# Token-mixer projections as pairs of seven block products in a one-core diffusion trunk layer

## What is computed

```python
h = rmsnorm(x, norm_mix) * (1.0 + sc1) + sh1          # sc1, sh1 ... from silu(cond) @ w_ada + b_ada
proj = h @ w_in                                       # 640 x 1024 by 1024 x 3584
xr, gr, q_raw, ff, fb, iv, og = split(proj)           # seven groups of 512 columns
...   # xr: convolution, two LRU scans;  q, ff, fb, iv, og: HGRN2, four heads of 128 columns, two directions
y = concatenate([y_lru, y_hg]) @ w_out
x = x + g1 * y
x = x + g2 * expert_choice_ffn(rmsnorm(x, norm_ffn) * (1.0 + sc2) + sh2)   # 16 experts, 3 x 4 MB of weights each
```

## Time and profile before

| what | value |
|---|---|
| median of 3 runs (lowest, highest) | 959.01 us (957.84, 960.46) |
| the profiled execution: its time, its span | 958.34 us, 956.6 us |
| DVE, ACT, POOL busy in the span | 54%, 30%, 11% |
| loads issued by SyncE and ScalarE | 253.77 MB on q1 of 276.15 MB in all |
| mean DMA rate over the span | 289 GB/s |

### The profile page before, as it was taken

One profiled execution on the slowest core, in us unless ns is written; L12 is line 12 of the kernel. 1 busy time (PEld: TensorE's weight loads), 2 busy tenths in 40 slices (PEclk: granted clock), 3 DMA queues, 4 the chain that ended last, 5 costly groups with the idle time before them and its releaser, 6 DMA issues.

```text
span 956.6 us, 19027 instructions
## 1 busy us (share of the span) xinstructions
PE 928.8 (97%) x8298; PEld 423.3 (44%) x8298; DVE 516.9 (54%) x1269; ACT 289.7 (30%) x507; POOL 101.2 (11%) x115
## 2 busy tenths in 40 slices
PE   5999999999999999999999999999999999999996
PEld 4555756768667554463222222222222223333332
DVE  4487667663654743764464461752636516444096
ACT  5137756564653824323020100200202002010103
POOL 3200010000000022112102002011020110100100
PEclk9999999999999999999999999999999999999999
DMA  9991014404029443168999999999999999999993
GB/s 333 334 386 52 2 55 157 160 5 176 10 92 367 174 164 150 66 240 323 403 399 404 408 416 408 415 401 413 418 405 413 405 413 425 401 426 413 412 380 122
DMA packets 52930, 276.15 MB, mean 289 GB/s; under 512 B 4400, under 2 KB 12752, under 8 KB 39920
## 3 DMA queue, kind: packets, MB, share of 16 engines
q1 hardware_dynamic: 45744, 253.77, 66.1%
q0 software_dynamic: 5584, 15.89, 5.7%
q10 hardware_dynamic: 1520, 5.28, 1.4%
HBM read 261.91 MB, written 13.01 MB: 287 GB/s over the span
## 4 chain that ended last, share of the span: by engine, by line
PE 79%; DMA 8%; DVE 5%; ACT 3%; issue 3%; POOL 0%; SPq 0%; POOLq 0%; DVEq 0%; ACTq 0%
PE pa L699 44%; PE p L699 34%; DMA ring<-in_w_up_dram 3%; DMA reg_e<-in_w_up_dram 3%; DMA ring<-in_w_ada_dram 1%; ACT reg_c L1374 1%; ACT L1374 1%; ACT reg_d L1374 1%; DMA reg_c<-h_rows,row_s 0%; ACT reg_b L1374 0%; DVE reg_a L2246 0%; DVE reg_b L1867 0%; PE p L854 0%; DVE reg_a L2241 0%; DVE reg_b L1838 0%
## 5 line engine op out<-in xcount | busy, mean ns | idle before, releaser
L699 PE MATMUL pa<-ring,reg_b 128*32 128x512 f32 (+1 forms) x1696 | 250.0, 593 | 0.7 <-DMA ring<-in_w_up_dram 0.5
L699 PE MATMUL p<-ring,reg_b 128*16 128x512 f32 (+1 forms) x1920 | 215.3, 592 | 1.1 <-issue 1.1
L699 PE MATMUL pa<-reg_a,ring 128*128 128x512 f32 (+1 forms) x640 | 191.2, 453 | 2.2 <-DVE reg_a L1730 1.5
L699 PEld LDWEIGHTS pa<-ring,reg_b 128*32 128x32 f32 (+1 forms) x1696 | 82.5, 117 | 143.7 <-issue 142.6
L699 PEld LDWEIGHTS pa<-reg_a,ring 128*128 128x128 f32 x640 | 98.3, 191 | 80.1 <-issue 79.9
L699 PEld LDWEIGHTS p<-ring,reg_b 128*16 128x16 f32 (+1 forms) x1920 | 63.9, 102 | 143.9 <-issue 143.9
L2142 DVE STREAM_TRANSPOSE reg_b<-reg_b 32x128 f32<-32x128 f32 x384 | 116.3, 303 | 5.9
L2158 DVE TENSOR_TENSOR reg_b<-reg_b,pa 128x512 f32<-128x512 f32 x16 | 11.0, 686 | 146.7 <-PE pa L699 146.4
L1374 ACT ACTIVATE reg_b<-pa 128x512 f32<-128x512 f32 (+1 forms) x20 | 12.4, 619 | 239.8 <-PE pa L699 239.8
L1374 ACT ACTIVATE reg_b<-reg_d,x_mod 128x128 f32<-128x128 f32 (+1 forms) x112 | 39.4, 440 | 140.7 <-PE p L699 140.7
L1374 ACT ACT_TABLE_LOAD x57 | 73.1, 1283 | 4.6 <-issue 2.8
(11 more groups left out here) (335 smaller groups left out, 937.4 us busy)
## 6 DMA issues: line engine op xcount, KB each, us to landing
ring<-in_w_gate_dram SPq DMA_DIRECT2D x25, 2048.0 KB, 21.1
ring<-in_w_down_dram SPq DMA_DIRECT2D x24, 2048.0 KB, 24.1
ring<-in_w_up_dram SPq DMA_DIRECT2D x22, 2048.0 KB, 21.5
ring<-in_w_ada_dram SPq DMA_DIRECT2D x8, 2048.0 KB, 8.5
ring<-in_w_in_dram SPq DMA_DIRECT2D x6, 2048.0 KB, 19.9
ring<-in_w_ada_dram SPq DMA_DIRECT2D x8, 1024.0 KB, 12.8
reg_a<-in_w_up_dram SPq DMA_DIRECT2D x4, 2048.0 KB, 20.3
reg_a<-in_w_gate_dram SPq DMA_DIRECT2D x3, 2048.0 KB, 18.1
```

The source lines that it names most:

```text
L699: return nc.tensor.matmul(out, lhsT, rhs, start=start, stop=stop, **kw)
```

## The change

- **Pairs.** The last two items of FILL[0] to FILL[5] (always feature items: Q and OG, or FF and FB) form a pair, `TWOS`. The pair's 256 columns, cut in two, by 1024 features, cut in two, and the 640 tokens, cut in two halves of 320, are multiplied as 2 x 2 blocks with seven products in place of eight (Winograd's form). A product is 4 matmuls of 320 columns into one PSUM bank, the first 320 of its 512 columns.
- **Token sums.** GpSimd makes four sums or differences of quarters of `hT` (128 x 1280 each), once, right behind its copy of the prompt tokens, which no longer waits behind the LRU state. They lie in slots 2 and 3 of the ring, which hold no weights of `w_in` any more.
- **Weight sums.** VectorE makes four of them a pair (128 x 512 each, SBUF to SBUF): those of pairs 0 and 1 behind the LRU's second scan, those of pair u + 2 at the end of unit u.
- **Joins.** ScalarE copies the first and second product (128 x 320 each, PSUM to SBUF) behind its logarithm. VectorE makes seven 320-wide adds: the first in front of the weighings, the other six behind them and ahead of the head's output, the ada bias, the state updates and the masks. Five of the seven read PSUM. In even units ScalarE then applies Silu in place, behind the key copy.
- **TensorE's order** in a pair: products 1 and 2, [first ada sum], 3, 4, 5, 6, [second ada sum and `turn_k`, in an order that depends on the unit], 7. The head norm of units 2 and 4 stands behind product 4. The `ada_turn` follows.
- **Values first.** EARLY is now the V item of head 1; FILL[1] keeps FF and FB, and in units 3 and 5 the V item comes in front of the pair.
- **Loads.** Those weights come as cells of 128 columns (0.5 MB, rows of 512 B) into slots 5, 0 and 1; each is used again when its column is free, and SyncE waits in between for TensorE's items and for earlier cells to land.
- The slot of `a2[0]` is moved, and two semaphores of the routing become one; nothing else behind unit 5 changes.

```diff
-         (("in", IN_Q), 5), (("in", IN_OG), 0), (("in", IN_FF), 1), (("in", IN_FB), 2), (("in", IN_V), 3)]
+         (("head", 5), 5), (("head", 0), 0), (("head", 1), 1), (("sums", 0), 2), (("sums", 1), 3)]
...
+HEAD0 = [(IN_Q, 0), (IN_OG, 0), (IN_FF, 0), (IN_FB, 0), (IN_V, 0)]
+EARLY = (IN_V, 1)
 FILL = []
 for _h in range(1, HEADS):
-    FILL += [[(IN_Q, _h), (IN_OG, _h)], [(IN_FF, _h), (IN_FB, _h), (IN_V, _h)]]
+    FILL += [[(IN_Q, _h), (IN_OG, _h)], ([(IN_V, _h)] if _h > 1 else []) + [(IN_FF, _h), (IN_FB, _h)]]
+TWOS = [fill[-2:] for fill in FILL]
 FILL += [[(IN_GR, 0), (IN_GR, 1)], [(IN_GR, 2), (IN_GR, 3)]]
-HEAD0 = [(IN_Q, 0), (IN_OG, 0), (IN_FF, 0), (IN_FB, 0), (IN_V, 0)]
-EARLY = FILL[1].pop(0)
...
+        mixing = ring[:, 2:4, :, :].rearrange("p s k n -> p (s k n)")
+        x_sum = [mixing[:, m * 4 * HALF:(m + 1) * 4 * HALF].rearrange("p (k t) -> p k t", k=4) for m in range(4)]
+        w_sum = [[mixing[:, 16 * HALF + (3 * b + m) * 512:16 * HALF + (3 * b + m + 1) * 512].rearrange("p (k n) -> p k n", k=4)
+                  for m in range(3)] for b in range(2)]
+        x_quarter = [[hT[:, 4 * kh:4 * kh + 4, HALF * th:HALF * (th + 1)] for kh in range(2)] for th in range(2)]
+        banks = [pa[n // 2][:, 512 * (n % 2):512 * (n % 2) + HALF] for n in range(4)]
...
+            for g in (IN_Q, IN_OG, IN_FF, IN_FB):
+                cell_load(g, 0)
+            sp_eng.wait_ge(freed[0], 1)
+            cell_load(IN_V, 0)
+            cell_load(IN_Q, 1)
+            cell_load(IN_OG, 1)
+            cell_load(IN_V, 1)
+            sp_eng.wait_ge(freed[1], 1)
+            cell_load(IN_FF, 1)
+            cell_load(IN_FB, 1)
+            cell_load(IN_Q, 2)
+            cell_load(IN_OG, 2)
+            whole_load("ada", 4)
+            sp_eng.wait_ge(full, 3)
+            cell_load(IN_FF, 2)
+            sp_eng.wait_ge(full, 4)
+            cell_load(IN_FB, 2)
+            sp_eng.wait_ge(full, 5)
+            cell_load(IN_V, 2)
+            sp_eng.wait_ge(full, 6)
+            cell_load(IN_V, 3)
+            whole_load("ada", 5)
+            whole_load("ada", 6)
+            sp_eng.wait_ge(two_ps, 7)
+            sp_eng.wait_ge(*cells_by((IN_V, 3)))
+            cell_load(IN_Q, 3)
+            cell_load(IN_OG, 3)
+            sp_eng.wait_ge(*cells_by((IN_OG, 3)))
+            cell_load(IN_FF, 3)
+            cell_load(IN_FB, 3)
+            for c in range(7, 12):
+                whole_load("ada", c)
+            whole_load("in", IN_GR)
+            whole_load("out", 0)
+            whole_load("out", 1)
...
             pool.wait_ge(h_mod, MIXED)
             pool.wait_ge(xt_dve, NT + MIXED)
             nc.gpsimd.tensor_copy(hT_p[:, :, :], hT[:, :, TS:T]).then_inc(pool_step, 1)
+            pool.wait_ge(freed[2], 1)
+            pool.wait_ge(freed[3], 1)
+            nc.gpsimd.tensor_tensor(x_sum[0], x_quarter[1][0], x_quarter[1][1], ALU.add).then_inc(mixed, 1)
+            nc.gpsimd.tensor_tensor(x_sum[2], x_quarter[0][0], x_quarter[1][0], ALU.subtract).then_inc(mixed, 1)
+            pool.wait_ge(mixed, 2)
+            nc.gpsimd.tensor_tensor(x_sum[1], x_sum[0], x_quarter[0][0], ALU.subtract).then_inc(mixed, 1)
+            pool.wait_ge(mixed, 3)
+            nc.gpsimd.tensor_tensor(x_sum[3], x_quarter[0][1], x_sum[1], ALU.subtract).then_inc(mixed, 1)
...
+            def product(i, bank, w, x):
+                for k in range(4):
+                    r = mm(banks[bank], w[:, k, :], x[:, k, :], k == 0, k == 3)
+                r.then_inc(two_ps, 1)
+            def two_start(i):
+                one, two = TWOS[i]
+                for g, h in (one, two):
+                    pe.wait_ge(*cells_by((g, h)))
+                pe.wait_ge(empty[0], (USE[one] + 1) // 2)
+                product(i, 0, w_cell(one)[:, 0:4, :], x_quarter[0][0])
+                pe.wait_ge(empty[1], USE[one] // 2)
+                pe.wait_ge(mixed, 4)
+                pe.wait_ge(two_add, weights_by(i))
+                product(i, 2, w_sum[i % 2][0], x_sum[0])
+            def two_middle(i):
+                product(i, 1, w_cell(TWOS[i][0])[:, 4:8, :], x_quarter[0][1])
+            def two_second(i):
+                product(i, 3, w_sum[i % 2][1], x_sum[1])
+            def two_third(i):
+                pe.wait_ge(two_cp, copied_by(i) + 2)
+                product(i, 2, w_cell(TWOS[i][1])[:, 4:8, :], x_sum[3])
+                product(i, 0, w_cell(TWOS[i][1])[:, 0:4, :], x_sum[2])
+            def two_last(i):
+                pe.wait_ge(two_add, joined_by(i) + 1)
+                product(i, 3, w_sum[i % 2][2], x_quarter[1][1])
+                pe.sem_inc(full, 2)
...
-            project_sample(FILL[0][0], range(0, 2))
+            two_start(0)
             lru_sum()
...
+            def unit_projections(u):
+                if len(FILL[u]) > 2:
+                    project(FILL[u][0])
+                if u > 0:
+                    two_start(u)
+                if u == 1 or u == 3 or u == 5:
+                    pe.wait_ge(sc_done, NSC * u)
+                    ada_sum(ADA_UNIT[u])
+                two_middle(u)
                 if u == 0:
                     pe.wait_ge(ln_log, 1)
-                elif u in ADA_UNIT:
-                    pe.wait_ge(sc_done, NSC * u)
-                if u in ADA_UNIT:
                     ada_sum(ADA_UNIT[u])
-                project_prompt(fill[0])
+                two_second(u)
+                if u == 2 or u == 4:
+                    head_norm(u // 2 - 1)
+                two_third(u)
+                if u == 2 or u == 4:
+                    turn_k(u)
+                    two_last(u)
+                    return
+                if u <= 1:
+                    ada_sum(ADA_UNIT[u] + 1)
+                    turn_k(u)
+                    two_last(u)
+                else:
+                    two_last(u)
+                    ada_sum(ADA_UNIT[u] + 1)
+                    turn_k(u)
+                ada_turn(ADA_UNIT[u])
...
+            def two_copy(i, step):
+                (one_a, one_b), (two_a, two_b) = two_out(TWOS[i][0]), two_out(TWOS[i][1])
+                act.wait_ge(two_ps, 7 * i + 1 + step)
+                A((one_a, two_b)[step], banks[2 * step], ACT.Copy).then_inc(two_cp, 1)
...
+                if len(fill) > 2:
+                    projected(fill[0])
+                if u < len(TWOS):
+                    two_copy(u, 0)
+                    two_copy(u, 1)
...
+                if u >= len(TWOS):
+                    projected(fill[1])
+                elif d == 0:
+                    for item in fill:
+                        n = USE[item]
+                        act.wait_ge(empty[n % 2], n // 2 + 1)
+                    for item in fill:
+                        dst = yT[:, LT + item[1], :] if item[0] == IN_OG else raw[item[1] % 2][2]
+                        A(dst, dst, ACT.Silu).then_inc(two_cp, 1)
...
+            def weight_sums(i):
+                one, two = TWOS[i]
+                for item in (one, two):
+                    dve.wait_ge(*cells_by(item))
+                if i >= 2:
+                    dve.wait_ge(two_ps, 7 * (i - 1))
+                t1, t2, t4 = w_sum[i % 2]
+                a, b, at = w_cell(one), w_cell(two), weights_by(i) - 4
+                V.tensor_tensor(t1, b[:, 0:4, :], a[:, 0:4, :], ALU.subtract).then_inc(two_add, 1)
+                V.tensor_tensor(b[:, 0:4, :], b[:, 4:8, :], b[:, 0:4, :], ALU.subtract).then_inc(two_add, 1)
+                dve.wait_ge(two_add, at + 1)
+                V.tensor_tensor(t2, b[:, 4:8, :], t1, ALU.subtract).then_inc(two_add, 1)
+                dve.wait_ge(two_add, at + 3)
+                V.tensor_tensor(t4, a[:, 4:8, :], t2, ALU.subtract).then_inc(two_add, 1)
...
                 lru_scan(j + 1)
+                if j == 0:
+                    weight_sums(0)
+                    weight_sums(1)
...
+            def two_sum(i, step):
+                (one_a, one_b), (two_a, two_b) = two_out(TWOS[i][0]), two_out(TWOS[i][1])
+                at = joined_by(i)
+                if step == 4:
+                    for dst, other in ((two_a, two_b), (two_b, one_b)):
+                        dve.wait_ge(two_add, at + (4 if dst is two_a else 5))
+                        V.tensor_tensor(dst, dst, other, ALU.add).then_inc(two_add, 1)
+                after, dst, src, bank = ((4, two_a, one_a, 3), (3, one_a, one_a, 1), (6, one_b, two_a, 0),
+                                         (5, two_a, two_a, 2), (7, one_b, one_b, 3))[step]
+                dve.wait_ge(two_ps, 7 * i + after)
+                if step == 0:
+                    dve.wait_ge(two_cp, copied_by(i) + 1)
+                else:
+                    dve.wait_ge(two_add, at + (6 if step == 4 else step))
+                V.tensor_tensor(dst, src, banks[bank], ALU.add).then_inc(two_add, 1)
+                if step == 2 or step == 4:
+                    dve.wait_ge(two_add, at + (7 if step == 4 else step + 1))
+                    dve.sem_inc(empty[step // 4], 1)
...
```

(21 more changed lines are left out.)

131 lines of the change are left out of this document (75 added, 56 removed).

## The result

The changed kernel took 970.36 us (median of 5, 969.34 to 971.80) beside 959.01 us (957.84 to 960.46) for the kernel before on the same chip: ratio 1.0116, 95% interval 1.0102 to 1.0130. It is 11.4 us slower, where 3.4 us faster was forecast; the time lies above the whole range. The profiled execution took 970.6 us against 958.34.

A forecast was written before the change was run, and what follows sets the result against it. TensorE, busy 97% of the span, was taken as the bound. +1.7 us at unit 0's end became -4.4 at unit 5's; plus 1.0 at the gate load, -3.4: 955.6 us against 959.01, range 953.5 to 958, chance 0.42.

The forecast's parts named there:

- the one on GpSimd: GpSimd's four token sums, 12.6 us from the end of the modulation on, needed some 60 us later: cost nothing.
- Rival C: GpSimd's sums slow VectorE's convolution beside them; 8.2 us reach the LRU chain, 5.7 beyond TensorE's delay: 961.3 us, chance 0.10.
- TensorE's saving: Seven 320-column products in place of eight full-width blocks: 2.1 us less a feature pair, 12.9 us over six pairs.
- In front of the norm sums: Two whole products and a value item ahead of the LRU's norm sums start those sums 2.5 us later.
- Unit 0: The first unit cannot use its saving, as the chain behind the norm sums has no hole: ends 1.7 us later.
- the wait for ScalarE's copies: In unit 0, products three and four of the second half wait some 4 us, hidden as the scores wait anyway.
- The joins: VectorE's 320-wide adds at 0.52 us; six behind the weighing, 3.1 us, delay odd units' first ada sum and head outputs.
- rival B: The six adds behind the weighing take 0.9 us each and hold up units 1, 3 and 5: +7.8, 963.4 us, chance 0.13.
- Units 1 to 5: The five units after the first take the shift at the end from +1.7 us to -4.4 us.
- Weight sums: VectorE's four a pair, 2.8 us; those of pairs 0 and 1 fit a 7.17 us idle time and cost nothing.
- Loads: Cells with 512 B rows move at 290 GB/s, in time; unit 1's ada load lands 1 us late.
- The wait of 1.0 us at the gate load: At unit 5's end TensorE waits 1.0 us for the gate projection's load: 9.1 us to land, 8.2 available.

The follow-up runs named there:

- run 1: The changed kernel with GpSimd's four token sums cut to 4 of 320 columns each, the other columns left out: 964.22 us, ratio 1.0053 to the kernel before.
- run 5: The changed kernel with the four token sums moved from GpSimd into VectorE's idle times, nothing left out: 962.71 us, ratio 1.0034 to the kernel before.
- run 2: The kernel before with eight unread GpSimd sums of 640 columns added, behind its prompt copy, which is moved earlier: 966.16 us, ratio 1.0071.
- run 7: Run 5 with only the first block product of unit 0 ahead of the LRU's norm sums, the second behind them: 961.11 us, ratio 1.0019.
- run 9: Run 5 with the moves of run 6, run 7 and run 8 all at once: 954.42 us, ratio 0.9953 to the kernel before.
- run 12: Run 10 with the load of the eighth block of modulation weights queued ahead of head 3's last four cells: 956.17 us, ratio 0.9965.
- run 4: The changed kernel with unread matmuls added in TensorE's two waits at the first gates: 967.74 us, ratio 1.0078 to the kernel before.
- run 6: Run 5 with unit 0's bias addition ahead of joins 1 to 4 and unit 1's modulation product one block product later: 963.99 us, ratio 1.0044.
- run 10: Run 9 with unit 1's modulation product put back behind the first two block products instead of three: 956.15 us, ratio 0.9957.
- run 11: Run 10 with ScalarE's two unit 0 copies ahead of its wait for the LRU's outputs, and the bias addition ahead of the last weighing: 957.48 us.
- run 8: Run 5 with the head's norm sums one block product earlier, ahead of product 4, in units 2 and 4: 959.31 us, ratio 0.9998.

## Why the prediction was wrong

**The step that failed** is the one on GpSimd: "needed only in front of the norm sums, some 60 us later: nothing". I priced when the results are needed, and not what the work itself does to a neighbour. It costs 7.3 us at head 0: runs 1 and 5 give all of it back, each in another way, and run 2 brings 6.3 of it into the kernel before. With the sums elsewhere the changed kernel is 3.8 us slower than before and not 11.4 (run 5). Rival C named this mechanism and had 0.10. It got the size wrong too: 12.6 less 4.43 of idle gave 8.2 on the chain, of which 5.7 was to show. TensorE's gates were left out of it: they wait for the first convolution and not for the last, so the idle time behind the convolution covers only 1.0 us of it (4.43 us before, 3.40 after), and the clock adds 2.0 us at head 0. The 2.5 us of TensorE's own delay stand behind it and are not shared (7.30 + 2.31 = 9.6 at the norm sums).

The page that I cited there (the Trainium skill, GPSIMD Engine Reference, Specifications) warns of the contention. Another one, with the sums' length of 3.1 us from my rows, would have given the size: by the Trainium skill, SBUF — State Buffer, Who interferes with whom, the port pair of the two engines is an exclusive lock, held for a whole instruction, while the other blocks. The trace agrees: 2.97 us for 0.35 us of work, beside sums of 2.9 to 3.2 us. By the same page a VectorE instruction with one input from SBUF is touched only in its fast mode; L1958 was (2.91 us), and its price does look like that mode: 0.55 us for 512 columns and 0.34 for 128 is 0.55 ns a column, where L1960 and L1961 (0.75 and 0.35) pay 1.04.

**TensorE's saving: right.** 336 instructions of 320 columns, a product in 2.15 to 2.17 us; 61.80 us an expert pair. The lines by form of the changed kernel:

```profile
L797 PE MATMUL pa<-ring 128*128 128x320 f32 x192 | 56.0, 444 | 4.2 <-ACT reg_b L1524 4.2
L797 PE MATMUL pa<-reg_a,ring 128*128 128x320 f32 x144 | 42.2, 436 | 0.9 <-ACT reg_d L1524 0.9
```
(336 by 0.271 is 91 us; the mean of one there includes the overlap with its neighbour.)

**In front of the norm sums: right**, 2.31 us for 2.5. Run 7 shows that it was a choice of order and not a cost of the products.

**Unit 0: wrong by 4.4 us.** There are two parts. The scores also wait for the bias of the modulation, which VectorE adds behind the last join. I had the joins "ahead of the state updates and the masks" and asked who waits for those; the addition at 152.49 stood in my own rows, inside that block, and I did not ask who waits for it. In the changed kernel, VectorE:

```profile
163.78 0.82 DVE L2057 SCALAR_TENSOR_TENSOR reg_d<-reg_d 128x640 f32<-128x640 f32 x1
164.51 0.48 DVE L2098 TENSOR_TENSOR reg_d<-reg_d,pa 128x320 f32<-128x320 f32 x1
...
167.45 0.49 DVE L2098 TENSOR_TENSOR reg_d<-reg_d,pa 128x320 f32<-128x320 f32 x1
168.08 0.24 DVE L1880 TENSOR_TENSOR mods<-p,bv 128x8 f32<-128x8 f32 x2
```
The bias addition is done 4.5 us behind the weighing that the scores need (163.78, 168.32); of that TensorE shows 2.83 us as a wait. The other 1.6: I called the wait for ScalarE's copies (4.18 us, predicted as 4) hidden by the scores' own, but what TensorE has behind it, down to the updates, ends only at 165.6, while VectorE's weighings, 22.0 us behind the norm sums as predicted, were there at 163.8. TensorE is late there by its clock: its two products behind the wait take 6.26 us at a granted clock of 0.61 (154 to 158 us), where in run 7, behind a wait of 2.04 us, the same two take 4.57:

```profile
143.90 4.57 PE L789 MATMUL pa<-ring 128*128 128x320 f32 x16 [2.04 <-ACT reg_b L1522]
```
A wait that was counted as hidden was so in its length, and not in what came behind it.

**The joins: size right, place wrong.** 0.49 us and with their handover 0.58, six in 3.6 us for the 3.1 predicted; rival B's price of 0.9 is refuted. But their place behind the weighings is on the path in unit 0 and at the end of unit 4, and in unit 1 once the rest is faster (0.64 us in run 9, 3.77 in run 12), which my list of who waits did not hold.

**Units 1 to 5: 144.7 us where the forecast had 142.7.** Unit 1 was better (26.1 for 27.9: no wait for weights, none at the outputs). Unit 3 was 0.6 and unit 5 0.7 us longer than forecast. The missed term is at the border of units 4 and 5: head 3's values go to the bank that the last join lets go, 1.92 us. The waits for the key copy in units 2 and 4 came as predicted in kind, 1.51 us each for 1.3.

**Weight sums: right**, in the hole for nothing, 2.11 us of which were left. **Loads: the rate was right.** In the stretch from 52 to 64 us the channels are full both with the cells' rows of 512 B (first window, the run with tiny sums) and with whole rows (second, the kernel before plus sums):

```profile
52.00:64.00 12.00, 12.00 (x49) 6.93 (x48) 9.30 (x20) 2.30 (x6) 1.04 (x5) 1.00 1.07 285
```
```profile
52.00:64.00 12.00, 12.00 (x49) 6.96 (x48) 9.60 (x6) 1.53 (x4) 11.53 (x8) 1.00 1.05 387
```
285 against 387 GB/s, and 290 was my estimate. The two rates in the rows, 356 and 386, taken as a fixed cost for each packet and a cost by size, give 308 for 512 B, so that part of the closeness is luck. As to the page, the Trainium skill (DMA: Bandwidth & Descriptors, Specifications) puts line rate already at 512 B, and here the measurement decides against it.

That the loads cost nothing in the changed kernel is because TensorE was late elsewhere: in unit 1 of runs 4, 6, 9, 10 and 11 the modulation's weights, queued behind four cells, are the wait that comes up next, 2.25 to 3.70 us. The wait of 1.0 us at the gate load did not come either: TensorE shows none at the end of unit 5, though only 8.4 us lie between the load's issue (306.54) and that end, 8.2 in the forecast; why the load was in time stays open.

**Behind unit 5** the changed kernel's profile is 1.1 us longer (653.97 us against 652.86). The profiles of all fourteen kernels, alike in that stretch but for small things, lie between 652.11 and 654.24 us there, so this needs no cause. I had read the big expert loads as beginning only behind the units; in fact the first is issued ahead of unit 5's end, 12.0 us before the change and 4.3 after it, which run 9 shares with its 652.49 us.

## What to carry to other kernels

Before work goes to an idle engine, look at what its neighbour executes in the same microseconds: beside a VectorE stage on the path, GpSimd work need not be free however late its result is needed, and here its long instructions cost each VectorE instruction the most. Where work is put "behind" something in a queue, list every instruction from there on with its waiter, the two-column one too, since it was a 0.24 us addition behind 3.6 us of joins that made TensorE wait 2.83 us. A wait that looks hidden can still lower the granted clock of what comes behind it (6.26 us for 4.57 here). And count on a chain of waits: here the same stretch was held in turn by a bias, a load behind cells and the same bias a unit on, so runs 6, 10, 11 and 12 moved the time by nothing that could be measured as a gain, while three moves at separate places made the version that beats both kernels, 954.4 us.

## What was not expected of the hardware

GpSimd and VectorE, both with work queued, take turns instruction by instruction: 128 columns on VectorE took 2.97 us beside sums of 1280 columns (2.9 to 3.2 us), 1.62 beside sums of 640 (1.7), and 0.80 beside copies of 640 (some 0.9 each, their own turns of waiting included), for 0.35 alone.

A stall can cost TensorE twice. Behind idle times of 2.5 to 3.7 us inside the units, the modulation's product took 3.27 to 3.60 us instead of 1.93 in runs 6 and 11; the scores of unit 1 took 3.33 instead of 2.16 in run 12, and those of unit 0 2.63 to 2.92 instead of 1.82 in runs 1, 5, 7 and 8, behind 2.10 to 4.52 us. Where it was slow, the granted clock over it was 0.50 to 0.58. In runs 9 and 10, with idle times of 3.06 and 2.78 us, the product kept its 1.93, and in the changed kernel the scores kept their 1.82 behind 2.83. So the same stall was seen with and without the loss, and these runs do not tell which it will be.
